# Hybrid GLA and attention layer with a 32-expert MoE: the first block's sums in PSUM banks of their own, and the rows of the first two blocks turned by TensorE

## The reference

```python
logits = (x2d @ w_router) + b_router            # 520 tokens, 32 experts
top_v, top_e = lax.top_k(logits, TOP_K)         # 4 experts per token
gates = jax.nn.softmax(top_v, axis=-1)
...
def expert_block(args):
    xb, e = args
    hh = xb @ w_up[e] + b_up[e]                 # (rows, 1024) x (1024, 2048)
    return clamped_swiglu(hh) @ w_down[e] + b_down[e]   # (rows, 1024) x (1024, 1024)
```

## Time and profile before

| | |
|---|---|
| median of 3 runs | 1406.92 us (1405.11 to 1406.96) |
| the profiled execution | 1409.57 us |
| its span, first to last instruction | 1407.8 us |
| mean granted TensorE clock | 0.982 |
| PE busy | 1340.0 us (95%) |
| DVE busy | 933.3 us (66%) |
| ACT busy | 193.3 us (14%) |
| POOL busy | 112.3 us (8%) |
| moved by DMA | 468.79 MB, 333 GB/s over the span |
| chain that ended last | PE 83%, DMA 9%, DVE 5% |

### The profile page before, as it was taken

How to read it: one execution, slowest core, us unless ns; L and a number is a source line. 1 busy time by engine, 2 the same in 40 slices (tenths; PEclk the granted TensorE clock), 3 DMA queues, 4 the chain that set the end, 5 groups by cost and what they waited for, 6 DMA issues and landing times.

```text
span 1407.8 us, 22270 instructions
## 1 busy us (share of the span) xinstructions
PE 1340.0 (95%) x6722; PEld 548.8 (39%) x6722; DVE 933.3 (66%) x2127; ACT 193.3 (14%) x385; POOL 112.3 (8%) x154
## 2 busy tenths in 40 slices
PE   8999999987898999998999999899999998999996
PEld 7866565553232333332333333233333332333332
DVE  3524247645776777776777777577787775778768
ACT  4231133421000000000000000000000000000012
POOL 3000000000000010000001000000100000010010
PEclk9999989999899999999999999999999999999998
DMA  9405162055699999999999999999999999999967
GB/s 362 112 6 180 31 209 105 31 206 219 262 411 422 421 383 422 393 422 421 421 386 413 392 418 421 422 420 380 421 390 415 404 420 421 420 375 423 388 254 300
DMA packets 90669, 468.79 MB, mean 333 GB/s; under 512 B 11878, under 2 KB 29016, under 8 KB 40226
## 3 DMA queue, kind: packets, MB, share of 16 engines
q1 hardware_dynamic: 74254, 441.43, 77.8%
q0 software_dynamic: 7440, 16.82, 3.1%
q10 hardware_dynamic: 8948, 10.19, 2.1%
HBM read 623.60 MB, written 28.51 MB: 463 GB/s over the span
## 4 chain that ended last, share of the span: by engine, by line
PE 83%; DMA 9%; DVE 5%; ACT 1%; issue 1%; SPq 0%; DVEq 0%; POOLq 0%; ACTq 0%
PE ps L1803 41%; PE ps L1822 21%; DMA raw<-in_w_down_dram 8%; PE ps L1505 5%; PE ps L1482 5%; PE ps L1709 4%; PE ps L1786 2%; DVE v_gate L1414 1%; DMA w_a_cols<-in_w_in_dram 1%; PE ps L1668 1%; PE ps L1667 1%; PE ps L1758 1%; DMA slot_outputs<-y_rows,out_idx 0%; DVE v_gate L1420 0%; DVE xT L1332 0%
## 5 line engine op out<-in xcount | busy, mean ns | idle before, releaser
L1803 PE MATMUL ps<-raw,xT 128*64 128x512 f32 x2944 | 656.5, 596 | 16.5 <-DMA raw<-in_w_up_dram 13.4
L1803 PEld LDWEIGHTS ps<-raw,xT 128*64 128x64 f32 x2944 | 206.2, 137 | 401.1 <-issue 357.7
L1822 PE MATMUL ps<-raw,aT 128*64 128x512 f32 x1440 | 319.5, 593 | 8.3 <-DMA raw<-in_w_down_dram 8.3
L1332 DVE STREAM_TRANSPOSE xT<-x_hold 32x192 f32<-32x192 f32 (+1 forms) x728 | 293.1, 403 | 51.4 <-PE ps L1803 31.3
L1332 DVE STREAM_TRANSPOSE aT<-act_g 32x256 f32<-32x256 f32 x360 | 228.6, 635 | 59.1 <-PE ps L1822 49.2
L1822 PEld LDWEIGHTS ps<-raw,aT 128*64 128x64 f32 x1440 | 102.0, 137 | 210.4 <-issue 185.8
L842 ACT ACTIVATE act_s<-act_g 128x512 f32<-128x512 f32 x46 | 29.0, 631 | 703.2 <-DVE act_g L1316 703.2
L501 POOL DMA_INDIRECT slot_outputs<-y_rows,out_idx x45 | 45.4, 1009 | 610.9 <-ACT y_rows L847 610.9
L1239 DVE TENSOR_REDUCE found<-ps 128x2 f32<-128x8 f32 x48 | 8.0, 167 | 121.9 <-PE ps L1758 121.9
L493 POOL DMA_INDIRECT x_rows<-expert_inputs,row_idx x48 | 49.3, 1027 | 361.6 <-DVE row_idx L1240 256.8
L1505 PE MATMUL ps<-w_c_cols,hT 128*128 128x512 f32 x128 | 59.6, 621 | 0.0
(11 more groups left out here) (353 smaller groups left out, 875.1 us busy)
## 6 DMA issues: line engine op xcount, KB each, us to landing
raw<-in_w_up_dram SPq DMA_DIRECT2D x368, 1024.0 KB
raw<-in_w_down_dram SPq DMA_DIRECT2D x184, 1024.0 KB
slot_outputs<-zeros ACTq DMA_DIRECT2D x1, 8320.0 KB, 28.1
raw<-slot_outputs SPq DMA_DIRECT2D x8, 1024.0 KB, 13.4
w_c_cols<-in_w_in_dram SPq DMA_DIRECT2D x1, 4096.0 KB, 33.7
w_out_sb<-in_w_out_dram SPq DMA_DIRECT2D x1, 4096.0 KB, 13.9
w_a_cols<-in_w_in_dram SPq DMA_DIRECT2D x1, 2624.0 KB, 13.5
x_sb<-in_x_prompt_dram SPq DMA_DIRECT2D x4, 512.0 KB, 5.6
```

Of the source, the lines that this page charges most:

```text
L1332: dve.transpose(dst_at(rows_out, group), src_at(rows_in, parity)).then_inc(done, 1)
L1803: ins = mm(ps[SUB * i:SUB * i + SUB, bank, :], xT[:, j, :], raw[:, SLOT[j], c:c + HF], start=False, stop=(j == UPU - 1))
L1822: ins = mm(ps[SUB * i:SUB * i + SUB, 2, :], aT[:, j, r, :], raw[:, SLOT[UPU + j], D * r + HF * i:D * r + HF * i + HF], start=False, stop=( ...
```

## The change

Block 0's first-layer sums go to banks 7 (gate) and 4 (linear); its bias is laid there before the table product, which itself moves from bank 6 to bank 1. One of the four keep-busy products goes. PE turns the rows of block 0 and of block 1, each with eight transposes in two groups of four, into banks 3 and 6; those of block 1 stand in PE's order ahead of the last unit of block 0. ACT copies the turned rows by quarters: those of block 0 into a new tile `xT_first`, those of block 1 into `xT`. `hold(1)` and DVE's turn of block 1 go. The lists of blocks 1 and 2 come after units 2 and 4 of block 0. In the loop the second part of the next block's turn stands between the clamp and the product, where it was at the beginning of the following turn of the loop, and ACT holds the block two ahead ahead of `y_out`. The gather of block 2 waits for PE's turn of block 1 in place of ACT's hold.

```diff
+        xT_first = R("xT_first", [P, UPU, SUB])
...
+        FIRST_BANKS, TURN_BANKS = (7, 4), (3, 6)
+        def turned(a, h):
+            return ps[0:SUB, TURN_BANKS[a], :].rearrange("p (c h s) -> p h c s", c=4, h=2)[:, h]
...
 def gather(b):
-                    if b == 1:
-                        pool.wait_ge(x0_psum, 1)
-                    if b > 1:
+                    if b in (1, 2):
+                        pool.wait_ge(x0_psum, 2 * b)
+                    if b > 2:
                         pool.wait_ge(x_held, b - 1)
...
@@ ACT @@
-            act.wait_ge(x0_psum, 1)
-            for h in range(2):
-                act.activation(xT[SUB * h:SUB * h + SUB], ps[0:SUB, 3:5, :].rearrange("p a (c h s) -> p h (a c) s", c=4, h=2)[:, h],
-                               ACT.Copy).then_inc(xT_ready, 8)
-            hold(1)
+            for b, dst in ((0, xT_first), (1, xT)):
+                for a in range(2):
+                    act.wait_ge(x0_psum, 2 * b + a + 1)
+                    for h in range(2):
+                        act.activation(dst[SUB * h:SUB * h + SUB, 4 * a:4 * a + 4], turned(a, h), ACT.Copy).then_inc(xT_ready, 4)
+            act.sem_inc(x_held, 1)
             sigmoid(0)
             hold(2)
...
             with act.Fori(1, nb) as b:
                 sigmoid(b)
+                hold(b + 2)
                 y_out(b - 1)
-                hold(b + 2)
...
@@ DVE; the copies of the table read bank 1 in place of bank 6 @@
             find_slots(own, 2)
-            indices(own, 2)
             dve.wait_ge(up_bias_done, 1)
             select(sel_up, 1, sel_up_ready)
             select(sel_dn, 0, sel_dn_ready)
+            dve.sem_inc(up_read, 1)
+            indices(own, 2)
             find_slots(own, 3)
-            turn_x(1, 0)
-            clamp(0)
+            dve.wait_ge(up_used, UPU)
+            dve.tensor_scalar(act_g[:], ps[:, FIRST_BANKS[0], :], LIMIT, None, ALU.min).then_inc(g_ready, 1)
+            own.do(dve.tensor_scalar(act_l[:], ps[:, FIRST_BANKS[1], :], LIMIT, -LIMIT, ALU.min, ALU.max))
             swiglu(own, 0)
...
             with dve.Fori(1, nb) as b:
-                turn_x(b, 1)
...
                 clamp(b)
+                turn_x(b + 1, 1)
                 swiglu(o, b)
...
-            dve.sem_inc(xT_ready, 8)
             turn_a(nb - 1, aT_last)
...
@@ PE @@
+            def turn_rows(b):
+                pe.wait_ge(gathered, 16 * b + 16)
+                for a in range(2):
+                    for c in range(4):
+                        ins = pe.transpose(ps[0:SUB, TURN_BANKS[a], P * c:P * c + P], x_rows[:, 4 * a + c:HF:UPU], ident[:])
+                    ins.then_inc(x0_psum, 1)
             find(0)
-            keep_busy(4)
+            keep_busy(3)
             pe.wait_ge(order_made, 1)
             mm(ps[:, 2, 0:NE], ones_f[0:NE, :], blocks_ahead[:], start=True, stop=True).then_inc(order_psum, 1)
-            pe.wait_ge(gathered, 16)
-            for c in range(UPU):
-                ins = pe.transpose(ps[0:SUB, 3 + c // 4, P * (c % 4):P * (c % 4) + P], x_rows[:, c:HF:UPU], ident[:])
-            ins.then_inc(x0_psum, 1)
+            pe.wait_ge(sel_up_ready, 1)
+            bias(FIRST_BANKS[0], 0, sel_up)
+            bias(FIRST_BANKS[1], FF, sel_up).then_inc(up_bias_done, 1)
+            turn_rows(0)
             pe.drain().then_inc(mixer_left, 1)
...
+            def first_up():
+                for j in range(UPU):
+                    if j in (0, 4):
+                        pe.wait_ge(xT_ready, 8 + 2 * j)
+                    if j == 7:
+                        turn_rows(1)
+                    up_unit(0, j, xT_first, FIRST_BANKS)
+                    if j in (2, 4):
+                        find(j // 2)
...
             table()
-            up(0)
+            first_up()
```

More of the change, by code:

```diff
@@ L1294, in _ @@
             dve.wait_ge(over_psum, 1)
-            step(dve.tensor_copy(blk_expert[:], ps[:, 6, 0:BLKS]))
-            step(dve.tensor_copy(blk_start[:], ps[:, 6, 2 * BLKS:3 * BLKS]))
-            step(dve.tensor_copy(blk_row[0:1, 0:2 * BLKS], ps[0:1, 6, 0:2 * BLKS]))
+            step(dve.tensor_copy(blk_expert[:], ps[:, 1, 0:BLKS]))
+            step(dve.tensor_copy(blk_start[:], ps[:, 1, 2 * BLKS:3 * BLKS]))
+            step(dve.tensor_copy(blk_row[0:1, 0:2 * BLKS], ps[0:1, 1, 0:2 * BLKS]))
             step(dve.tensor_copy(blk_row[0:1, 2 * BLKS:2 * BLKS + 1], blk_cols[0:1, 3:4]))
@@ L1769, in _ @@
             ins.then_inc(pos_psum, 1)
-            find(0)
-            keep_busy(4)
-            pe.wait_ge(order_made, 1)
-            mm(ps[:, 2, 0:NE], ones_f[0:NE, :], blocks_ahead[:], start=True, stop=True).then_inc(order_psum, 1)
-            pe.wait_ge(gathered, 16)
-            for c in range(UPU):
-                ins = pe.transpose(ps[0:SUB, 3 + c // 4, P * (c % 4):P * (c % 4) + P], x_rows[:, c:HF:UPU], ident[:])
-            ins.then_inc(x0_psum, 1)
[L1778 to L1782, removed]
             def bias(bank, c0, sel):
@@ L1788, in bias, with table, up_unit @@
                 return ins
+            def turn_rows(b):
[4 more added lines that the diff above has]
+                    ins.then_inc(x0_psum, 1)
+            find(0)
+            keep_busy(3)
+            pe.wait_ge(order_made, 1)
+            mm(ps[:, 2, 0:NE], ones_f[0:NE, :], blocks_ahead[:], start=True, stop=True).then_inc(order_psum, 1)
+            pe.wait_ge(sel_up_ready, 1)
+            bias(FIRST_BANKS[0], 0, sel_up)
+            bias(FIRST_BANKS[1], FF, sel_up).then_inc(up_bias_done, 1)
+            turn_rows(0)
+            pe.drain().then_inc(mixer_left, 1)
+            def table():
+                pe.wait_ge(over_made, 1)
+                mm(ps[:, 1, 0:3 * BLKS], ones_f[:], blk_diag[:].rearrange("p a b -> p (a b)"), start=True, stop=True).then_inc(over_psum, 1)
+            def up_unit(b, j, rows_in, banks):
+                pe.wait_ge(landed[j], 16 * b + 16)
+                for bank in range(2):
+                    for i in range(2):
+                        c = FF * bank + HF * i
+                        ins = mm(ps[SUB * i:SUB * i + SUB, banks[bank], :], rows_in[:, j, :],
+                                 raw[:, SLOT[j], c:c + HF], start=False, stop=(j == UPU - 1))
+                ins.then_inc(up_used, 1)
+            def first_up():
[7 more added lines that the diff above has]
+                        find(j // 2)
             def up(b):
                 pe.wait_ge(sel_up_ready, b + 1)
-                if not (isinstance(b, int) and b == 0):
-                    pe.wait_ge(up_read, b)
+                pe.wait_ge(up_read, b)
                 bias(0, 0, sel_up)
@@ L1798, in up @@
                 for j in range(UPU):
[L1799 to L1809, removed]
+                    up_unit(b, j, xT, (0, 1))
+                    if j == 3:
                         find(b + 2)
```

## The result

The changed kernel took 1399.6 us (median of 5 runs, 1398.49 to 1400.57) beside 1406.92 us for the one before (5 runs, 1404.44 to 1409.22): ratio 0.994, 95% interval 0.9929 to 0.9952, so 6.8 to 10.0 us faster. The forecast was 1395.7 us, range 1393.0 to 1399.8, a gain of 11.2 us. A later comparison of the same two kernels gave 0.9935 (0.9922 to 0.9948). The profiled execution of the changed kernel took 1399.04 us with a span of 1396.9, 10.9 us less than the traced span of before.

The account below looks back on a forecast made before the run. The weight stream was taken to bound the expert loop, but PE's chain its start. 1.46 - 0.9 + 7.8 (hole) + 3.07 (clock) - 0.2 (stream) = 11.2 us off the 1406.92 median gave 1395.7 us, range 1393.0 to 1399.8.

Parts of the forecast that it names:

- Start of block 0: Start-up on PE: one warming product fewer (0.9 us) and bias moved into a wait (0.55 us), 1.46 us earlier.
- Copies by quarters: ScalarE's copies of turned rows: four take about 1.6 us instead of 1.21, covered by the table product, cost zero.
- PE's turn of block 1: Inside block 0: eight transposes add 0.9 us to PE; gather lands in time, else PE held 1.0 or 2.2 us.
- Loop entry: PE entering the loop before block 1, reading the block count: 0.4 us, bounded by 0 and some 3 us.
- Block 1: Its first-layer matmuls start at 350.2 instead of 358.52, 8.3 us earlier, as DVE's turning leaves the hole.
- the clock's term: PE in block 1: shorter pause keeps the clock at 1.00 instead of 0.50, 21.6 us for the block, gaining 3.07.
- The weight stream: Loop's first weight loads on the DMA queues: issued at 353.5 and 375.1, stream just fits, 0.2 us deducted.
- The loop and the last block: DVE's moved turn costs zero in the loop; last block's extra 2.5 us reaches the end as zero, bound 2.5.
- A: Start-up hole: late rows, loop entry or low clock keep part; gain 5 to 9, 1398 to 1402 us; chance 0.14.
- C: DVE in the loop: moved turn delays each second layer, 44 us per microsecond beyond the slack, slower; chance 0.03.
- D: End of the kernel: the last block's full 2.5 us reach the end, 1398.2 us, in range; no separate chance.
- B: Weight stream gives gain back: small form 9.5 us gain, 1397.4; bound throughout, gain near 0, 1407, chance 0.03.

Follow-up runs that it names:

- the filled pause: Kernel before the change plus seven keep-busy products in PE's pause between the first layers of blocks 0 and 1, results unused: ratio 0.9982 (0.9972 to 0.9992).

## Why the prediction was right, and where it was off

It forecast faster, and the time lies in its range, 3.9 us above the single value and 0.2 below the upper end. There is some luck in this: the summed gain of 11.2 us lies outside the measured 6.8 to 10.0, and the upper end of the range came from the bounds of the gather and of the loop entry, neither of which cost anything. Step by step:

- *Start of block 0.* Forecast 333.9, traced 333.98. The bias gives its 0.55 (0.48 measured). The 0.9 us for the warming product was read from one execution; three of the four traces of that start bear it out, and in the fourth, and in the run with the old start, it was nothing.
- *Copies by quarters.* Four took 1.58 us (forecast 1.6), done before they were wanted.
- *PE's turn of block 1.* Forecast 0.9 on its path, the chain has 1.02; the gather was in time, and its lateness never came up in a trace.
- *Loop entry.* Forecast 0.4, measured nothing: the bias follows the last unit in the same instant. The fetch stall that the Trainium skill, "Runtime: NRT & Kernel Launch", section Instruction fetch mechanics, made possible does not show at this entry. Whether the entry takes a branch of that kind at all, no run here shows.
- *Block 1.* Forecast 350.2, traced 350.19, and the filled pause shows the clock's term alone: 2.4 to 2.8 us of the 3.07.
- *The weight stream.* This is the term that was mis-sized. The first load at 353.5 (traced 353.71) and the next at 375.1 (375.20) were right, but I let the stream run at 421 GB/s from the first moment and so found it just able to follow, deducting 0.2 us. At that rate the 21.4 us between the two issues would carry 9.0 MB; by windows laid between them it carried 8.4 to 8.5 MB in three of five traces and 8.0 and 8.1 in the others, where eight units, without gather and scatter, are 8.39. So the stream was still behind with the first expert when the next load was issued, and from there to the end of the first piece it moved 26.9 to 28.0 MB where before it moved 26.5. The first piece ended 67.9 to 69.8 us after block 2 (67.6 and 67.8 before), latest in the two traces with 8.0 and 8.1 MB: 0 to 2 us were given back, about 1 in the middle.
- *The loop and the last block* at zero: shown, by the period, by the kernels without the loop's part, and by 32.8 us from the first weighing to the end. The last second layer did start the 2.5 us later that were forecast.
- *From the traces to the median.* Before and after, the first traces have mixers of equal length (the last product of the mixer ends the same, at 313.1). Their spans differ by 10.9 us, near the sum of 11.2, but this pair is a favourable one: over all traces it is 8.6 us behind block 0's start (forecast 9.8) and 0.4 to 1.6 ahead of it (forecast 1.46). The runs gave 7.3 us by the first medians and 8.9 by the second. That their mixers vary by some 4 us is enough to cover what is still missing, but no run shows that it is this. I took the sum off a median of three runs of before; in 29 runs beside the first experiments its median was 1408.16.

Rivals A (a part stays in the hole), C and D are refuted by the trace. B in its small form (1.7 us) came near in size, about 1 us, but not in its way: the next load was issued in time, and it was the bytes still outstanding that came late.

## What to carry to other kernels

Where a hole at the start of a loop has the engine, its clock and the weight stream idle at once, each has to be followed separately to the first place where another resource takes over. The stream passed on about 1 us less than PE had gained: in the first microseconds it was below its full rate, and then had no gap in which to catch up. Before working out a term from one trace, look at whether it hangs on the moment at which the granted clock rises: in a second trace of the same kernel one of the terms here was gone. The same code can also end a stall 2 us earlier or later, so that an effect of 1 us needs more than one trace. And compare executions from a marker behind the noisy stage, here block 0's first matmul, when the runs spread as widely as the effect.

## What the hardware showed unexpectedly

The stage ahead of block 0, the same in four kernels here, ended between 331.1 and 335.7 us, nearly the whole spread of the runs. What makes it vary was not tried. The weight stream moved 0.2 to 0.3 MB in the 2 us after its first issue and 0.8 in the next 2 (381 to 426 GB/s), both in the first trace of before and in five with the changed kernel's loads. By an estimate from this some 1.4 us pass until the bytes come, and the 186 GB/s above are mostly that. What differed between executions of the same loads were the first 8 us as a whole: 346 to 355 GB/s in three traces, 289 and 307 in the two whose first piece ended latest. A PE loop entered without any wait showed no gap at all at its entry.
